# The first block's z projection in three half-precision products, its weights split by GpSimd

## The reference, cut to what matters

```
xn   = rms_norm(h, pre_mix_norm)
proj = xn @ w_in                      # 1024 x 3336
z, xbc, dt = split(p_ssd, [512, 1536])
xbc  = silu(causal_conv(xbc));  xs, B, C = split(xbc)
y    = ssd_chunked(xs * softplus(dt), ..., B, C) + d_skip * xs
y    = y * silu(z)                    # then a norm per group, then w_out
```

## Time and profile before

| | us |
|---|---|
| median of 3 runs | 740.94 (739.91 to 741.89) |
| profiled execution | 741.43 |
| its span (first to last instruction) | 739.6 |
| around the span | 1.8 |
| PE busy | 730.2 (99%) |
| DVE busy | 563.0 (76%) |
| ACT busy | 434.7 (59%) |
| POOL busy | 47.2 (6%) |

### The profile page before, as it was taken

One profiled execution on the slowest core, in us unless ns is written; L12 is line 12 of the kernel. 1 busy time (PEld: TensorE's weight loads), 2 busy tenths in 40 slices (PEclk: granted clock), 3 DMA queues, 4 the chain that ended last, 5 costly groups with the idle time before them and its releaser, 6 DMA issues.

```text
span 739.6 us, 16490 instructions
## 1 busy us (share of the span) xinstructions
PE 730.2 (99%) x7072; PEld 597.5 (81%) x7072; DVE 563.0 (76%) x893; ACT 434.7 (59%) x690; POOL 47.2 (6%) x81
## 2 busy tenths in 40 slices
PE   9999999999999999999999999999999999999997
PEld 7888877889778888888877696898888888865553
DVE  5699976777879999997668797889685666762453
ACT  5599872523667676666556573387483755653342
POOL 0000133040020000000002000003003000000000
PEclk9999999999999999999999999999999999999999
DMA  9990303512575566546680743339326254566001
GB/s 318 398 400 5 113 18 140 206 38 81 178 278 184 180 207 228 214 173 242 239 331 5 284 168 115 115 116 341 114 102 241 86 213 171 215 228 226 31 0 58
DMA packets 67146, 129.43 MB, mean 175 GB/s; under 512 B 3969, under 2 KB 28033, under 8 KB 66817
## 3 DMA queue, kind: packets, MB, share of 16 engines
q1 hardware_dynamic: 66032, 126.07, 47.3%
q0 software_dynamic: 320, 1.61, 0.6%
q10 hardware_dynamic: 720, 0.70, 0.3%
HBM read 127.32 MB, written 1.05 MB: 174 GB/s over the span
## 4 chain that ended last, share of the span: by engine, by line
PE 83%; DVE 8%; ACT 4%; DMA 2%; SPq 2%; issue 1%; ACTq 0%; DVEq 0%
PE bank L623 38%; PE bank L746 13%; PE bank L3207 11%; PE bank L2533 3%; PE bank L1571 3%; DMA ring<-in_w_in_dram 2%; PE bank L1552 2%; DVE arena L569 2%; SPq L494 1%; PE bank L1834 1%; PE bank L900 1%; PE bank L1887 1%; DVE arena L1082 1%; PE bank L2014 1%; DVE arena L611 1%
## 5 line engine op out<-in xcount | busy, mean ns | idle before, releaser
L623 PE MATMUL bank<-hg,arena 128*128 128x256 f16 x2496 | 275.0, 273 | 0.2 <-DVE hg L648 0.2
L623 PEld LDWEIGHTS bank<-hg,arena 128*128 128x128 f16 x2496 | 243.8, 98 | 30.7 <-issue 1.1
L569 DVE SCALAR_TENSOR_TENSOR arena<-ring,arena 128x1024 f16<-128x1024 f32 x150 | 175.6, 1226 | 58.4 <-ACT arena L537 58.4
L537 ACT ACTIVATE arena<-ring 128x1024 f16<-128x1024 f32 x150 | 146.6, 1044 | 87.6 <-PE bank L3207 37.6
L3207 PE MATMUL bank<-arena 128*128 128x512 f16 (+1 forms) x480 | 83.6, 336 | 0.0
L3207 PEld LDWEIGHTS bank<-arena 128*128 128x128 f16 x480 | 47.0, 98 | 36.1
L746 PE MATMUL bank<-arena 128*128 128x256 f16 x528 | 57.8, 273 | 0.0
L746 PEld LDWEIGHTS bank<-arena 128*128 128x128 f16 x528 | 51.7, 98 | 6.0
L556 DVE SCALAR_TENSOR_TENSOR arena<-ring,arena 128x2048 f16<-128x2048 f32 x22 | 50.4, 2292 | 0.7
L746 PE MATMUL bank<-mix,arena 128*128 128x256 f16 x384 | 42.2, 273 | 0.0
L549 ACT ACTIVATE arena<-ring 128x2048 f16<-128x2048 f32 x22 | 41.7, 1894 | 0.0
(11 more groups left out here) (420 smaller groups left out, 978.0 us busy)
## 6 DMA issues: line engine op xcount, KB each, us to landing
ring<-in_w_in_dram SPq DMA_DIRECT2D x12, 2048.0 KB, 9.0
ring<-in_ffn_w_up_dram SPq DMA_DIRECT2D x22, 1024.0 KB, 7.4
ring<-in_w_ff_dram SPq DMA_DIRECT2D x8, 2048.0 KB, 9.2
ring<-in_w_ff_dram SPq DMA_DIRECT2D x16, 1024.0 KB, 6.5
ring<-in_ffn_w_down_dram SPq DMA_DIRECT2D x11, 1024.0 KB, 6.3
ring<-in_w_out_dram SPq DMA_DIRECT2D x8, 1024.0 KB, 7.3
ring<-in_w_xk_dram SPq DMA_DIRECT2D x2, 2048.0 KB, 10.7
ring<-in_w_xv_dram SPq DMA_DIRECT2D x2, 2048.0 KB, 10.2
```

The lines of the kernel that those rows point to most:

```text
L537: nc.scalar.activation(quarter(halves_of(chunk)[0], chunk, q), quarter(slot(*chunk), chunk, q), ACT.Copy, scale=W_SCALE).then_inc(*mark("w ...
L569: nc.vector.scalar_tensor_tensor(quarter(halves_of(chunk)[1], chunk, q), quarter(slot(*chunk), chunk, q), W_SCALE, quarter(halves_of(chunk ...
L623: mm = nc.tensor.matmul(out_, weight[a][:, k, cols], src[:, k, b, :], start=(first and i == 0), stop=(last and i == 2), skip_group_check=True)
```

## The change

The z tiles become `product3` like the others. Their halves are made by POOL alone (`pool_z`): for each of the four tiles of 128 x 1024 weights it scales them by 64 in place, copies them into f16 (high) and subtracts to get the low half, each step waiting for the one before. Tile 0's halves go to the upper half of xk, those of tiles 1 to 3 into the ring slot itself, over the source of the tile before. `pool_z` stands behind the pad's clearing and ahead of `pool_ssd`.

`product3` reads `pre16` in xv, so xv must live until the last z tile. XDT, XDEC and ST, which lay in xv, move to hg, whose f32 activations nobody reads any more. Two waits follow: the first halves of `w_out` that go to hg wait for the SSD's last product instead of the last z tile, and the second half of `mem16` waits for the first z tile, since it takes the place of tile 0's halves in xk.

```diff
@@ views
-        XDT = xv[:, 0, :].rearrange("p (c d) -> p c d", c=NC_)
-        XDEC, ST = xv[:, 1, 0:SSD_D], xv[:, 1, SSD_D:2 * SSD_D]
+        XDT = hg[:, 0:4, :].rearrange("p k t -> p (k t)").rearrange("p (c d) -> p c d", c=NC_)
+        XDEC = hg[:, 4:6, :].rearrange("p k t -> p (k t)")
+        ST = hg[:, 6:8, :].rearrange("p k t -> p (k t)")
@@ wout_high
-                    act.wait_ge(*at("proj1", 12))
+                    act.wait_ge(*at("ssd y", 1, 1))
@@ pe_z_tile
-            if j == 0:
-                chunk_ready(pe, "w_in", "z")
             if j % 2 == 0:
                 pe.wait_ge(*at("proj1 out", b - 4))
+            pe.wait_ge(*at("z low", j))
             for k in range(KT):
-                mm = nc.tensor.matmul(halves(b % 4)[:, i % 2, :], slot("w_in", "z")[:, k, j * P:(j + 1) * P],
-                                      hg[:, k, :], start=(k == 0), stop=(k == KT - 1))
+                mm = product3(halves(b % 4)[:, i % 2, :], z_halves(j), k, slice(0, P), pre16, k == 0, k == KT - 1)
+            if j == 0:
+                mm.then_inc(*mark("proj1_z", "first z tile"))
@@ new functions
+        def z_source(j):
+            return slot("w_in", "z")[:, :, j * P:(j + 1) * P]
+
+        def z_halves(j):
+            if j == 0:
+                v = xk[:, 4:8, :].rearrange("p a b -> p (a b)").bitcast(F16).rearrange("p (w k n) -> p w k n", w=2, k=KT)
+                return [v[:, a] for a in range(2)]
+            v = ring[:, CHUNK_NO[("w_in", "z", 0)] % RING, :].bitcast(F16).rearrange("p (k n) -> p k n", k=KT)
+            at_ = 2 * P * (j - 1)
+            return [v[:, :, at_ + P * a:at_ + P * a + P] for a in range(2)]
+
+        def pool_z(pool):
+            pool.wait_ge(*at("chunk", CHUNK_NO[("w_in", "z", 0)]))
+            for j in range(4):
+                if j:
+                    pool.wait_ge(*at("z low", j - 1))
+                nc.gpsimd.tensor_scalar(z_source(j), z_source(j), W_SCALE, None, ALU.mult).then_inc(
+                    *mark("z_weights_scaled", "z scaled", j))
+                pool.wait_ge(*at("z scaled", j))
+                nc.gpsimd.tensor_copy(z_halves(j)[0], z_source(j)).then_inc(*mark("z_weights_high", "z high", j))
+                pool.wait_ge(*at("z high", j))
+                nc.gpsimd.tensor_tensor(z_halves(j)[1], z_source(j), z_halves(j)[0], ALU.subtract).then_inc(
+                    *mark("z_weights_low", "z low", j))
@@ act_mem_gain
+            if ms[0]:
+                act.wait_ge(*at("first z tile"))
@@ the list of GpSimd
             pool_project1(pool)
+            pool_z(pool)
             pool_ssd(pool)
```

## The result

The changed kernel takes 752.93 us (median of 4 runs, 752.56 to 753.59) against 740.59 for the kernel before: 1.0166 of it, 95% interval 1.0150 to 1.0182, 12.3 us slower. 756.4 was forecast, 746 to 764 as the range. The profiled execution took 753.59 us, with a span of 751.8.

The account below looks back on a forecast made before the run. PE, busy 99%, was taken as the bound, with DVE and ACT nearly level between 52 and 90 us. Port +14.7, PE's saving -0.95 and clock +1.7 made +15.4 us on the profiled 741.43; forecast 756.4, range 746 to 764.

Parts of the forecast that it names:

- The port: From 52 us, POOL's SBUF reads hold DVE's two-input instructions: 15.4 us held, 14.7 after 0.7 of DVE work running beside POOL.
- PE's saving: At the z tiles, f16 halves save PE 0.98 us a tile; only tile 3's counts, so the end comes 0.95 us earlier.
- Where it falls: From 52 to near 73 us, eight POOL instructions come between DVE's eight shifts, leaving DVE some 12 us late after them.
- Nothing catches up before 89.15: Between the shifts and 89.15 us, DVE's and ACT's mutual waits move along, so the whole 14.7 us is carried through.
- PE's two idle times: PE sits idle before L1653 and before L1664, some 14 us in all, most of it the first time.
- The clock: After PE's second idle time TensorE may run at half clock for 3.4 us: 1.7 us added, bounds 0 and 3.4.
- A: Rival: DVE keeps the port, POOL enters only where DVE is off it or waits; DVE loses 8.2 us, 750; chance 0.12.
- B: Rival: only POOL's two-input subtractions collide with DVE; +7.5 us, 748; chance 0.06.
- C: Rival: POOL's one-input instructions hold the port nearer 1.5 us than 0.9; 4.8 us more, 761; chance 0.18.
- D: Rival: DVE's loss falls into unseen slack or POOL barely holds the port; 740.0 or 737.0 us; chance 0.12.

Follow-up runs that it names:

- POOL's work alone: Kernel before, f32 z tiles kept, plus POOL's twelve instructions writing halves nobody reads; PE's first z tile waits for the last: 752.25 us, ratio 1.0152.
- the products alone: Changed kernel without POOL's twelve instructions; z tiles still f16 matmuls, on ready finite values: 739.89 us, ratio 0.9994 to the kernel before.
- tile 3 alone: Changed kernel with POOL's scaling, cast and subtraction for z's tile 3 only; tiles 0 to 2 f16 on ready values: 743.99 us, ratio 1.0042.
- without the scaling and with PE kept at work: Changed kernel without POOL's four scalings, plus 66 and 10 filler matmuls ahead of two PE waits: 751.13 us, ratio 1.0131 to the kernel before.
- The kernel with PE kept at work: Changed kernel plus filler matmuls, 66 ahead of PE's wait at L1693 and 14 ahead of L1215's: 751.70 us, ratio 1.0137 to the kernel before.

## Why the prediction was right, and where not

**The port** was right as the cause: with POOL's work alone the loss is there, with memsets in its place it isn't, and with casts in place of the subtractions it shrinks. The term was 15.4 us less 0.7. It measured 13.1: the subtraction 1.87 and not 2.05 (the turns of the earlier trace rows had given 1.8), one input 0.78 and not 0.9, and one cast almost free. The 0.78 is under the bound of 0.84 that I had taken from the MEMSETs: a MEMSET's length was no bound for how long a reading instruction holds DVE. (The copy of 128 elements is 0.075 over the MEMSETs' line and not 0.10, which changes nothing in the sum.)

**PE's saving** was right for tiles 0 to 2, which only lengthen a wait, and wrong for tile 3, which was to bring 0.95. DVE's L1152 is 0.7 us less late than L1323, and the next instruction, L1491, loses 0.7 to POOL's L2290, which it now meets earlier. With the products alone it loses 0.9. With f32 tiles and POOL's work the first stretch of the table is as long as with f16 tiles: the term is nil, and by the same port.

**Where it falls** was wrong. The step "in turns, eight POOL instructions come between eight shifts", some 12 us late at their end, failed: three met them, for 3.4 us, and the shifts took 6.7. The reason is the scaling, 2.8 us long with 0.8 on the port; I had taken the time on the port for the whole length. Without the scaling the turns are what I described, 13.8 us for the eight. What DVE loses in sum hardly changed by it, since each POOL instruction still met DVE once, only later.

**"Nothing catches up before 89.15"** failed in the changed kernel, for about 1.5 us, and with it the reading that a delay of DVE "has no cushion over half a microsecond": DVE had waited for ACT at two places of the kernel before, and the later losses ate these waits. DVE's timeline in the kernel before:

```profile
68.92 0.28 DVE L1165 TENSOR_SCALAR arena<-arena 8x256 f32<-8x256 f32 x1 [0.83 <-ACT arena L1142]
77.04 2.56 DVE L1117 SCALAR_TENSOR_TENSOR arena<-arena,params 128x256 f32<-128x256 f32 x6 [0.67 <-ACT arena L1107]
```

And in the changed kernel, where the first of them is gone (so is the second):

```profile
80.80 0.27 DVE L1192 TENSOR_SCALAR arena<-arena 8x256 f32<-8x256 f32 x1
```

I had the trace to see them, and looked only at PE's waits. Where the whole loss comes at the shifts or right behind them, ACT behind them is as late as DVE, and the waits move along: with tile 3 alone nothing was made up, and without the scaling and with PE kept at work (78.79 and 86.92 above) DVE lost 10.5 us and still waits 0.72 and 0.67. So it matters where a loss falls, and not only how large it is. This also closes the account of the kernel without the scaling: of the 2.5 us that DVE saved there, about 1.3 went into waits that stayed, and the half clock took 1.8.

**PE's two idle times** became one long one. As the shifts were late by little, PE came to L1682 with 0.29 us of waiting, and stood 7.98 at L1693: 8.3 in all and not some 14.

**The clock.** That an idle time of PE can be followed by half clock was right, and with tile 3 alone and without the scaling it cost 1.7 and 1.8 us. In the changed kernel, for which the 1.7 was forecast, it cost nothing that the rows show: the dip from 72 to 79 fell in the wait and beside DVE's lateness, and the one from 96 to 99.4, which I had not foreseen, slowed tile 2 by 1.3 us. The kernel with PE kept at work has neither (its one dip, from 64 to 68, doesn't show in the length) and takes as long up to that instruction.

The sum, from DVE's first shift to L1559: 13.1 of DVE, less 1.5 of waits, less tile 3's 0.7, plus 0.7 at L1491, make 11.6 (57.5 against 45.9). The execution was 0.3 ahead at 52 us, and another 0.9 arises behind the table's second stretch, which is as long as before; this makes the 12.2 us by which the span is longer. What makes the 0.9 I have not settled. The forecast of +15.4 had 1.6 too much for the port, 1.7 for a clock that cost nothing, 1.5 for the waits and 0.3 for the start; tile 3's 0.95, which didn't come, and the open 0.9 lie on the other side. So the cause and most of the size are right, and that the error is only 3.3 us is in part luck.

The rivals: A has DVE lose 8.2 us, 9.0 with its other terms, and is refuted by the turns without a scaling; B (7.5 us; by its own terms 7.4) is refuted by the casts' 0.78. C is right that the scaling is long, and wrong that this costs: both one-input instructions hold DVE for 0.8. D's slack is there, 1.5 us of it.

## What to carry to other kernels

An idle engine is not free when it shares a port with the one that sets the time: read what its instructions would hold, one by one, from the engine beside it, and not from their own length. Look for such meetings in work that the change only moves, too. If the same work can be done by the busy engine in one fused instruction, compare: here DVE's 1.22 us a tile (with one more instruction on ACT) stood against 3.4 us that it lost to POOL. And before an idle time of TensorE is counted as harmless, look at what it does right behind it.

## What the runs showed of the hardware

- POOL's scaling of 1024 f32 elements takes 2.8 us in place and out of place, and holds DVE for 0.8 us at its start only. A cast to f16 takes 1.12 us when it needn't wait and costs DVE 0.78.
- A DVE instruction with one SBUF input can be held too: L1749, a TENSOR_SCALAR of 4 elements from SBUF to SBUF, takes 0.17 us in the kernel before, 0.88 behind a scaling, 1.98 (the row at 64.02 above) inside a subtraction, and 0.56 beside a memset, which holds none of the instructions with two SBUF inputs. I had excluded only what reads a bank, and called this one "a tiny one". The Trainium skill (SBUF, section "Who interferes with whom") counts `tensor_scalar` among the operations that can take the shared port pair in a 2-port mode; the rows agree with it.
- The same section of the Trainium skill has the holder keep the pair for its whole instruction. For the subtraction that is near (2.18 us long, 1.87 lost), for the scaling it isn't (2.82 and 0.8).
- TensorE's dips to half clock come and go where two kernels don't differ: the kernel that scales out of place has one from 71 to 81 us, the changed one from 72 to 79 and again at 96 and 123. They do so between executions of one kernel as well. Of 23 executions of the kernel before, the twelve with a mean granted clock of 0.996 or 0.997 took 741.4 to 742.5 us, and ten of the eleven with 0.998 or 0.999 took 739.7 to 740.7. So 2 us between two such kernels are not the edit's until the clock rows have been read, and a stretch that holds the change says more than the whole time.
